# Experts' weights: six places of each kind, down weights asked for behind the next block's gate weights; turned rows and outcome in the table of constants

## What is computed

```python
for i in range(DEPTH):                      # attention, memory attention, feed-forward
    x = x + rms_norm(o, g_mix_post[i]);  x = x + rms_norm(f, g_ffn_post[i])
x = x + merged @ w_out[l]                   # RWKV-7 and latent attention, gated
h2 = rmsnorm(x, ffn_norm_g[l])
# hier_moe: top-1 of 4 groups, top-2 of its 8 experts; tokens sorted by expert
xb = x_pad[tok_buf].reshape(n_blocks, EXPERT_BLOCK, D)
def expert_block(args):
    xblk, e = args
    gt, up = jnp.split(xblk @ w_gu[e], 2, axis=-1)       # w_gu[e]: 1024 x 512
    return (jax.nn.silu(gt) * up) @ w_down[e]            # w_down[e]: 256 x 1024
yb = lax.map(expert_block, (xb, blk_expert)).reshape(P, D)
out = jnp.zeros((N + 1, D), h.dtype).at[tok_buf].add(yb * w_buf[:, None])
x = x + out;  return rmsnorm(x, final_norm_g)
```

## Time and profile before

| what | us |
| --- | --- |
| timed runs, median of 3 | 2247.7 |
| profiled execution, its own time | 2244.0 |
| its span, first to last instruction | 2242.2 |
| first block's rows turned (start of x(0)) | 1948.9 |
| end of the last block's down(15) | 2209.8 |

### The profile page before, as it was taken

How to read it: one execution, slowest core, us unless ns; L and a number is a source line. 1 busy time by engine, 2 the same in 40 slices (tenths; PEclk the granted TensorE clock), 3 DMA queues, 4 the chain that set the end, 5 groups by cost and what they waited for, 6 DMA issues and landing times. The chain is left out here.

```text
span 2242.2 us, 29227 instructions
## 1 busy us (share of the span) xinstructions
PE 2028.1 (90%) x12216; PEld 1427.7 (64%) x12216; DVE 1044.0 (47%) x1913; ACT 621.0 (28%) x1180; POOL 100.0 (4%) x119
## 2 busy tenths in 40 slices
PE   8989999999999799999999888887999999688883
PEld 4466688888855575788888776766656667433331
DVE  2276554446344764554554555555254543511113
ACT  1165222223221563322232233343143221000001
POOL 0000000000000000000000000111000000011102
PEclk9999999999999999999999989999999999799897
DMA  8100245322222100332322131000111234589995
GB/s 279 53 23 1 76 164 212 132 94 96 83 103 85 39 1 1 113 113 76 113 76 103 58 121 50 3 2 3 59 57 34 79 113 160 225 338 413 411 410 191
DMA packets 114533, 266.86 MB, mean 119 GB/s; under 512 B 9015, under 2 KB 71838, under 8 KB 105886
## 3 DMA queue, kind: packets, MB, share of 16 engines
q1 hardware_dynamic: 108062, 250.24, 30.5%
q0 software_dynamic: 5760, 12.59, 1.6%
q10 hardware_dynamic: 576, 2.10, 0.2%
HBM read 258.62 MB, written 27.26 MB: 128 GB/s over the span
## 5 line engine op out<-in xcount | busy, mean ns | idle before, releaser
L237 PE MATMUL ps<-arena 64*64 64x64 f32 (+11 forms) x6448 | 875.7, 355 | 112.5 <-DMA arena<-in_moe_w_gu 34.0
L237 PEld LDWEIGHTS ps<-arena 64*64 64x64 f32 (+3 forms) x6448 | 465.9, 152 | 483.9 <-issue 359.6
L247 PE MATMUL ps<-arena 128*128 128x128 f32 (+3 forms) x1182 | 162.9, 283 | 47.9 <-DVE arena L859 18.1
L395 DVE TENSOR_SCALAR arena<-arena 128x1024 int32<-128x1024 int32 (+1 forms) x204 | 138.1, 677 | 144.1 <-PE ps L243 83.4
L247 PEld LDWEIGHTS ps<-arena 128*128 128x128 f32 (+3 forms) x1182 | 135.2, 150 | 96.2 <-issue 48.4
L241 PE MATMUL ps<-HTr,WH1r 128*128 128x512 f32 (+1 forms) x448 | 169.9, 379 | 1.2 <-ACT T16r L1046 1.2
L241 PE MATMUL ps<-HTr,WH0r 128*128 128x512 f32 (+1 forms) x448 | 169.9, 379 | 1.2 <-ACT T16r L1046 1.2
L402 ACT ACTIVATE WH0r<-arena 128x1024 fp32r<-128x1024 f32 x86 | 91.4, 1063 | 213.6 <-DVE slot2r L398 92.3
L243 PE MATMUL ps<-T16r,WH0r 128*128 128x512 f32 (+1 forms) x384 | 144.0, 375 | 0.0
L243 PE MATMUL ps<-T16r,WH1r 128*128 128x512 f32 (+1 forms) x384 | 144.0, 375 | 0.0
L402 ACT ACTIVATE WH1r<-arena 128x1024 fp32r<-128x1024 f32 x82 | 87.2, 1063 | 197.4 <-DVE slot0r L398 106.3
(11 more groups left out here) (371 smaller groups left out, 2815.4 us busy)
## 6 DMA issues: line engine op xcount, KB each, us to landing
arena<-in_moe_w_gu SPq DMA_DIRECT2D x32, 2048.0 KB, 15.3
arena<-in_w_gate_up SPq DMA_DIRECT2D x44, 1024.0 KB, 7.1
arena<-in_moe_w_down SPq DMA_DIRECT2D x32, 1024.0 KB, 16.7
arena<-in_w_down SPq DMA_DIRECT2D x8, 2048.0 KB, 8.0
arena<-in_w_in SPq DMA_DIRECT2D x7, 2048.0 KB, 9.4
arena<-in_w_in SPq DMA_DIRECT2D x9, 1024.0 KB, 5.4
arena<-in_w_o SPq DMA_DIRECT2D x4, 2048.0 KB, 7.9
arena<-in_w_down SPq DMA_DIRECT2D x4, 1536.0 KB, 6.7
```

Of the source, the lines that this page charges most:

```text
L237: return e.matmul(o, l, r, start=start, stop=stop, skip_group_check=True)
L247: return e.transpose(o, i, ident[0:n, 0:n])
L395: e.tensor_scalar(h.bitcast(I32), raw.bitcast(I32), -4096, None, ALU.bitwise_and).then_inc(*v_half.up(*name, "mask"))
```

## The change

`RING` is 6 for both kinds of weights, where it was 5. The sixth gate place is `HTf`, the turned normed input that the router's matrix multiplications read; the sixth down place lies at column 10368, over the router's small buffers. The turned rows `XTm` and the outcome `YB0`, which lay in `HTf`, move over the table of constants behind its first 128 columns, and `YB1` takes the third place of gathered rows, so `XG` has two places. Gate weights of block n + 1 are asked for ahead of the down weights of block n. The rest of the diff writes `RING` for 5 and 2 for 3 in the same expressions of `p_expert_up`, `p_expert_down` and `p_expert_x`.

```diff
+        RING = 6
+        d_gat = [mark(f"rows{i}_in", queue, 16) for i in range(2)]
         WGU = [place("GU0", 16384, 4096), place("GU1", 8192, 4096), place("GU2", 12288, 4096),
-               at("GU3", 15360, 4096), at("GU4", 20480, 4096)]
-        WDN = [at(f"DN{x}", c, 2048) for x, c in enumerate((0, 6272, 2048, 4096, 8320))]
-        XG = [at("XG0", 25600, 1024), PB2, at("XG2", 24576, 1024)]
-        YB = [place(f"YB{q}", 6144 + 1024 * q, 1024) for q in range(2)]
-        XTm = [place(f"XTm{q}", 4096 + 1024 * q, 1024)...
+               at("GU3", 15360, 4096), at("GU4", 20480, 4096), HTf]
+        WDN = [at(f"DN{x}", c, 2048) for x, c in enumerate((0, 6272, 2048, 4096, 8320, 10368))]
+        XG = [at("XG0", 25600, 1024), PB2]
+        YB = [place("YB0", top + P + 2048, 1024), at("YB1", 24576, 1024)]
+        XTm = [place(f"XTm{q}", top + P + 1024 * q, 1024)...
...
         def s_gate_up(e, u):
-            if u >= 5:
-                e.wait_ge(*p_mo["up", (u - 5) // 2])
+            if u >= RING:
+                e.wait_ge(*p_mo["up", (u - RING) // 2])
...
             for u in range(2, 5):
                 s_gate_up(e, u)
                 s_down(e, u)
+            e.wait_ge(*p_ro["lg", 3])
+            s_gate_up(e, 5)
+            e.wait_ge(*v_ro["eb"])
+            s_down(e, 5)
 
         def s_experts(e, n):
+            for m in [n + 1] if n not in (15, NB - 1) else []:
+                for u in (2 * m, 2 * m + 1):
+                    if u >= RING:
+                        s_gate_up(e, u)
             for u in (2 * n, 2 * n + 1):
-                if u >= 5:
+                if u >= RING:
+                    s_down(e, u)
+
+        def s_more_experts(e, n):
+            if n == 16:
+                for u in (32, 33):
                     s_gate_up(e, u)
-            for u in (2 * n, 2 * n + 1):
-                if u >= 5:
-                    s_down(e, u)
+            s_experts(e, n)
 
         def g_rows(e, n):
-            if n >= 3:
-                e.wait_ge(*p_mo["xT", n - 3, 1])
-            e.indirect_dma_start(XG[n % 3], ...
+            if n >= 2:
+                e.wait_ge(*p_mo["xT", n - 2, 1])
+            e.indirect_dma_start(XG[n % 2], ...
...
-            for n in range(n0, min(n0 + 3, n1)):
+            for n in range(n0, min(n0 + 2, n1)):
                 rows and rows(e, n)
...
-                    if rows and n + 3 < n1:
-                        rows(e, n + 3)
+                    if rows and n + 2 < n1:
+                        rows(e, n + 2)
...
-            experts(e, (), expert=s_experts)
+            experts(e, (), expert=s_more_experts)
```

More of the change, by code:

```diff
@@ L2388, in build @@
         p_mo, v_mo, a_mo = mark("moe_bank", pe), mark("moe_step", vec), mark("moe_moved", act)
-        d_gu = [mark(f"gate_up{i}_in", queue, 16) for i in range(5)]
-        d_dn = [mark(f"down{i}_in", queue, 16) for i in range(5)]
-        d_gat = [mark(f"rows{i}_in", queue, 16) for i in range(3)]
+        RING = 6
+        d_gu = [mark(f"gate_up{i}_in", queue, 16) for i in range(RING)]
+        d_dn = [mark(f"down{i}_in", queue, 16) for i in range(RING)]
+        d_gat = [mark(f"rows{i}_in", queue, 16) for i in range(2)]
         d_y = [mark(f"block{i}_out", queue, 16) for i in range(2)]
         WGU = [place("GU0", 16384, 4096), place("GU1", 8192, 4096), place("GU2", 12288, 4096),
-               at("GU3", 15360, 4096), at("GU4", 20480, 4096)]
-        WDN = [at(f"DN{x}", c, 2048) for x, c in enumerate((0, 6272, 2048, 4096, 8320))]
-        XG = [at("XG0", 25600, 1024), PB2, at("XG2", 24576, 1024)]
-        YB = [place(f"YB{q}", 6144 + 1024 * q, 1024) for q in range(2)]
-        XTm = [place(f"XTm{q}", 4096 + 1024 * q, 1024).rearrange("p (k t) -> p k t", k=8) for q in range(2)]
+               at("GU3", 15360, 4096), at("GU4", 20480, 4096), HTf]
+        WDN = [at(f"DN{x}", c, 2048) for x, c in enumerate((0, 6272, 2048, 4096, 8320, 10368))]
+        XG = [at("XG0", 25600, 1024), PB2]
+        YB = [place("YB0", top + P + 2048, 1024), at("YB1", 24576, 1024)]
+        XTm = [place(f"XTm{q}", top + P + 1024 * q, 1024).rearrange("p (k t) -> p k t", k=8) for q in range(2)]
+        assert CONST["ident"] == (0, P) and P + 3072 <= NCONST
         ACTB, THm = [[at(f"{n}{q}", c + 256 * q, 256) for q in range(2)] for n, c in (("ACTB", 12928), ("THm", 13952))]
@@ L2414, in s_gate_up @@
         def s_gate_up(e, u):
-            if u >= 5:
-                e.wait_ge(*p_mo["up", (u - 5) // 2])
-            e.dma_start(WGU[u % 5].rearrange("p (k n) -> p k n", k=8), expert_weights(e, Wgu, u // 2, u % 2)).then_inc(
-                *d_gu[u % 5].up(u))
+            if u >= RING:
+                e.wait_ge(*p_mo["up", (u - RING) // 2])
+            e.dma_start(WGU[u % RING].rearrange("p (k n) -> p k n", k=8), expert_weights(e, Wgu, u // 2, u % 2)).then_inc(
+                *d_gu[u % RING].up(u))
         def s_down(e, u):
-            if u >= 5:
-                e.wait_ge(*p_mo["down", (u - 5) // 2])
-            e.dma_start(WDN[u % 5].rearrange("p (k n) -> p k n", k=2), expert_weights(e, Wdn, u // 2, u % 2)).then_inc(
-                *d_dn[u % 5].up(u))
+            if u >= RING:
+                e.wait_ge(*p_mo["down", (u - RING) // 2])
+            e.dma_start(WDN[u % RING].rearrange("p (k n) -> p k n", k=2), expert_weights(e, Wdn, u // 2, u % 2)).then_inc(
+                *d_dn[u % RING].up(u))
         def s_first_experts(e):
@@ L2439, in s_first_experts @@
                 s_down(e, u)
+            e.wait_ge(*p_ro["lg", 3])
+            s_gate_up(e, 5)
+            e.wait_ge(*v_ro["eb"])
+            s_down(e, 5)
         def s_experts(e, n):
+            for m in [n + 1] if n not in (15, NB - 1) else []:
+                for u in (2 * m, 2 * m + 1):
+                    if u >= RING:
+                        s_gate_up(e, u)
             for u in (2 * n, 2 * n + 1):
-                if u >= 5:
+                if u >= RING:
+                    s_down(e, u)
+        def s_more_experts(e, n):
+            if n == 16:
+                for u in (32, 33):
                     s_gate_up(e, u)
-            for u in (2 * n, 2 * n + 1):
-                if u >= 5:
-                    s_down(e, u)
+            s_experts(e, n)
         def g_rows(e, n):
-            if n >= 3:
-                e.wait_ge(*p_mo["xT", n - 3, 1])
-            e.indirect_dma_start(XG[n % 3], None, hn_scr, bass.IndirectOffsetOnAxis(ap=IDX[:, n:n + 1].bitcast(U32), axis=0),
-                                 bounds_check=S - 1, oob_is_err=False).then_inc(*d_gat[n % 3].up(n))
+            if n >= 2:
+                e.wait_ge(*p_mo["xT", n - 2, 1])
+            e.indirect_dma_start(XG[n % 2], None, hn_scr, bass.IndirectOffsetOnAxis(ap=IDX[:, n:n + 1].bitcast(U32), axis=0),
+                                 bounds_check=S - 1, oob_is_err=False).then_inc(*d_gat[n % 2].up(n))
         def p_expert_x(e, n):
-            xg = XG[n % 3]
+            xg = XG[n % 2]
             for hf in range(2):
                 bk = bank(e, ("xT", n, hf), v_mo, ("xT", n, hf))
-                e.wait_ge(*d_gat[n % 3][n])
+                e.wait_ge(*d_gat[n % 2][n])
                 for k in range(4):
@@ L2472, in p_expert_up @@
             bk = bank(e, ("up", n), v_mo, ("a", n))
-            w = [WGU[(2 * n + x) % 5].rearrange("p (k n) -> p k n", k=8) for x in range(2)]
+            w = [WGU[(2 * n + x) % RING].rearrange("p (k n) -> p k n", k=8) for x in range(2)]
             for u in (2 * n, 2 * n + 1):
-                e.wait_ge(*d_gu[u % 5][u])
+                e.wait_ge(*d_gu[u % RING][u])
             e.wait_ge(*v_mo["xT", n, 1])
@@ L2499, in p_expert_down @@
             t.then_inc(*p_mo.up("aT", n))
-            w = [WDN[(2 * n + x) % 5].rearrange("p (k n) -> p k n", k=2) for x in range(2)]
+            w = [WDN[(2 * n + x) % RING].rearrange("p (k n) -> p k n", k=2) for x in range(2)]
             for u in (2 * n, 2 * n + 1):
-                e.wait_ge(*d_dn[u % 5][u])
+                e.wait_ge(*d_dn[u % RING][u])
             for h in range(2):
```

## The result

The changed kernel takes 2273.26 us (median of 4 runs, 2269.72 to 2276.58) where the kernel before takes 2246.84 on the same chips: a ratio of 1.012, with a 95% interval of 1.0097 to 1.0143. It is slower by about 26 us. The profiled execution has a span of 2268.8 us, and its own time is 2270.58.

A forecast was written before the change was run, and what follows sets the result against it. The prediction took the weight stream to bound the experts' stage before the change, and late rows after it: loop +27.2, start +2.5 and tail -3.6 gave +26.1 us, so 2274 us, range 2245 to 2302.

The forecast's parts named there:

- The mechanism: In the experts' loop, rows asked for one block later land late, so TensorE waits for rows; 2.1 us more per period.
- The signs: Expected in the trace: row waits of 3 to 6 us in some 12 periods, gathers landing after 8 to 12 us.
- The start: Ahead of x(0), the first gather runs through gate weights 5 and lands after 7.0 us; +2.5 us for all blocks.
- The period: One block of the experts' loop, down to down: 8.75 us plus the gather's landing of 9.7, so 18.45 for 16.36.
- Waits of over 2.5 us: In the experts' loop, TensorE waits behind which the clock was said to fall, costing up 1.7 us.
- The deciding point: The gather's landing time in the loop: slower if over 8.2 us, faster if under 7.1.
- The tail: From the end of down(13) to that of down(15): 17.3 us where it was 20.9, so -3.6.
- The rival of the full price: In the loop, rows land as late as before, 14.9 us: +94, 2342; chance 0.12 for all beyond 2302.
- the row at 2190.6: Outcome written near the stage's end, 7.7 us to landing; used to bound the gather's landing between 7.7 and 11.8.
- The fast rival: In the loop, rows stay in time (landing up to 6.6 us) and weights stay the bound: -23, 2225; chance 0.10.
- the clock in a wait: In the loop, a lower clock after waits ahead of x and down: 13 x 1.7 = +22 on top, 2296.

The follow-up runs named there:

- the first experiment: The changed kernel with rows asked for in the order of the kernel before, still two places of rows and six of weights; 2222.74 us, ratio 0.9907.

## Why the prediction came out

The time was 2273.3 for 2274 predicted. The direction and its cause were foreseen; that the number agrees within 1 us is luck, since two errors in the loop cancel.

- **The mechanism** was right: thirteen waits for rows in front of the transposes, none for weights, a DMA share of 0.90 where I had about 0.89, a filled stretch from 1971 on. Undoing the late request alone turns +26 into -21. The signs were drawn too narrow: the waits are 2.3 to 8.1 us long for the 3 to 6 named, and the gathers landed after 6.0 to 11.8 for 8 to 12, six of the thirteen in less than the 7 us that I had named as a sign of being wrong.
- **The start**: x(0) at 1951.51 for 1948.89, +2.6; predicted +2.5. The first gather landed after 7.2 us; I took 7.0.
- **The period**: from 1978.80 (the request for down weights 6, at the end of down(0)) to the end of down(13), 2214.22 + 3.65 = 2217.87, are 239.1 us for 13 periods, 18.39 each; predicted 18.45. The parts are worse. The rows landed after 8.2 us on the mean (median 7.1), where I took 9.7, the middle of 7.7 and 11.8: 1.5 too high. But from the landing to the end of down passed 7.2 (18.39 less 3.0 and 8.2) for the 5.75 I had, 1.45 more, through the clock that falls in the wait: ten transposes took up to 2.37 us for 1.40, and down 3.7 to 5.4 for 3.65. I had priced that at 1.7 and put it with a rival, outside the sum. The two errors cancel. "Waits of over 2.5 us" was also no good mark for it: in the kernel before, up took 8.78 behind a wait of 2.08, and in the first experiment 7.09 behind one of 2.71.
- **The deciding point** was therefore wrong: I had the change at most even for a landing of 8.2 or less. At 8.2 it is 26 us slower; without the clock it would have been 13 x (16.94 - 16.36) - 1.1, or +6.
- **The tail**: 2217.9 to 2235.8 are 17.9 us; predicted 17.3, before 20.9.
- **The rival of the full price** was put aside because a period of 23.65 us holds only 16.4 of DMA work. That reasoning is wrong. In the kernel with the late rows alone the period is about 24.9 (1969.95 to 2293.3 for 13), the DMA engines are 0.69 busy and the rows land after 14.2 all the same, beside weights asked for in one lump just ahead of them. What kept the change from it is the new order of requests together with the sixth place. I had written that the order gives nothing in the loop; with six places it is worth 82 us once the rows are late. I had used its effect in choosing the row at 2190.6 (two down units asked for at that moment), but not seen it as the condition of the forecast.
- **The fast rival** had nearly the right price, by another way. With the rows early, 21 us are won, where I had 23 for a stream that starts earlier; the rows need not land within 6.6 us for it, only be asked for a block sooner (the variant with halved requests has them landing after 9.9 to 11.0, and nobody waits). Its working doesn't add up by the prediction's own terms: a period of 15.3 gives 13 x (15.3 - 16.36) - 1.1, or -15. The first experiment's period is 14.65 (1972.6 to 2163.1 for 13), which gives -23.

## What to carry to other kernels

When a ring loses a place, ask first which request really needs it: here the request could keep its old position in the queue, and only the shortened look-ahead of the loop cost time. A small indirect DMA on the chain is priced by what is asked for just ahead of it, not by the mean load; keep large requests away from it, or give it a lead that is longer than its landing behind them (here 25 us for 15). And a term that one shifts to a rival (the clock in a wait) still belongs in the sum if its condition is met by the forecast itself.

## What the runs showed of the hardware

- A gather of 128 rows of 4 KB took 4.5 us to land with little else underway, 14.2 beside gate weights in 16 KB pieces asked for just ahead, with the engines 0.69 busy over the stage, and 10.8 beside the same weights in 8 KB pieces.
- In one kernel the same gather landed after 10.7 to 11.8 us where it was issued 8 to 12.4 us behind the last gate weights, and after 6.0 to 7.1 at 16.3 us or more behind them.
- Gate weights in 8 KB pieces streamed as fast as in 16 KB pieces: 2222.6 against 2222.7 us for the whole kernel.
- Filling a wait of TensorE kept its clock up (ten transposes in 1.40 us for 2.40) and yet won nothing: the next rows landed later, 9.1 us on the mean for 8.2.
